# A hybrid mixer and product-key expert block on one Trainium2 core: segments of 1, 2, 2, 3 tiles, eight gather slots, other V rows on TensorE, and a segment's opening among the queries of the one before

## The reference, cut to what matters

```python
h = rmsnorm(x, norm_mix)
gq, gk, gv, gr, ga, sq, sk, sv = split(h @ w_in)
y_gla = gla_branch(gq, gk, gv, gr, ga) @ w_gla_out      # gated linear attention, chunks of 64, state carried
y_swa = swa_branch(sq, sk, sv, sinks) @ w_swa_out       # window of 2 chunks, 16 heads, ALiBi, sinks
gates = sigmoid(h @ w_branch_gate + b)                  # two gates of width 1024
x = x + (g_gla * y_gla + g_swa * y_swa) @ w_out
h = rmsnorm(x, norm_ffn)
q = (h @ w_q)                                           # 8 heads x 2 halves of 128
scores = q . sub_keys                                   # 128 keys in each half
top 16 of each half, top 16 of the 16 x 16 sums -> expert numbers e, gates g = softmax
x = x + sum over 8 heads x 16 experts of g * gelu(h . u_tab[e]) * v_tab[e]
x = x + sigmoid(rmsnorm(x) @ w_ple_gate) * (p @ w_ple_proj)
return rmsnorm(x, norm_final)
```

## Time and profile before

| | us |
|---|---|
| median of 3 runs (3624.73 to 3629.0) | 3628.56 |
| the profiled execution | 3617.58 |
| its span | 3615.5 |
| TensorE, VectorE, ScalarE, GpSimd busy | 2923.2, 2506.4, 1421.8, 1249.0 |
| first gather issued | 233.5 |
| `ysum` of the eight tiles added | 835, 1212, 1630, 2030, 2430, 2830, 3230, 3571 |

### The profile page before, as it was taken

How to read it: one execution, slowest core, us unless ns; L and a number is a source line. 1 busy time by engine, 2 the same in 40 slices (tenths; PEclk the granted TensorE clock), 3 DMA queues, 4 the chain that set the end, 5 groups by cost and what they waited for, 6 DMA issues and landing times.

```text
span 3615.5 us, 35606 instructions
## 1 busy us (share of the span) xinstructions
PE 2923.2 (81%) x11272; PEld 1953.4 (54%) x11272; DVE 2506.4 (69%) x5309; ACT 1421.8 (39%) x3619; POOL 1249.0 (35%) x1028
## 2 busy tenths in 40 slices
PE   8869988869887789587898789787877788686865
PEld 6767766746564456364576456464444455353423
DVE  0155666697778877689777986688666756677773
ACT  2223454233434443344443453344433543334532
POOL 0012222224343444344334443343433433333441
PEclk9989999988999899798899899899998998798988
DMA  6588878979999999999999999999999999999996
GB/s 221 177 334 337 340 315 328 365 305 422 421 421 420 414 390 420 421 393 398 400 421 421 420 403 405 403 414 390 421 421 421 421 421 421 419 398 412 413 421 248
DMA packets 198988, 1388.12 MB, mean 384 GB/s; under 512 B 22657, under 2 KB 24577, under 8 KB 35090
## 3 DMA queue, kind: packets, MB, share of 16 engines
q0 software_dynamic: 147456, 1073.81, 72.3%
q1 hardware_dynamic: 51346, 312.04, 21.8%
HBM read 1368.99 MB, written 16.78 MB: 383 GB/s over the span
## 4 chain that ended last, share of the span: by engine, by line
PE 34%; DMA 32%; DVE 17%; issue 8%; ACT 7%; POOL 2%; SPq 0%; DVEq 0%; POOLq 0%; ACTq 0%
DMA uv<-in_uv,idx 30%; PE bank L540 12%; PE bank L550 9%; PE ysum L728 8%; DVE acc L1241 4%; DVE uv L1218 4%; POOL uv L497 2%; DVE lidx L1077 2%; PE bank L609 2%; DVE vals L1074 1%; ACT bufX L804 1%; DMA slab<-in_slabs 1%; DVE bufE L1071 1%; DMA out<-bufA 1%; PE bank L529 1%
## 5 line engine op out<-in xcount | busy, mean ns | idle before, releaser
L497 POOL DMA_INDIRECT uv<-in_uv,idx x1024 | 1248.8, 1220 | 2299.3 <-PE ysum L728 1061.3
L1218 DVE SCALAR_TENSOR_TENSOR uv<-uv,hbuf 128x1024 f32<-128x1024 f32 x1024 | 1246.2, 1221 | 564.4 <-DMA uv<-in_uv,idx 544.7
L728 PE MATMUL ysum<-uv,diag 128*128 128x512 f32 x2232 | 1169.7, 666 | 402.8 <-ACT diag L974 396.2
L728 PEld LDWEIGHTS ysum<-uv,diag 128*128 128x128 f32 x2232 | 449.1, 211 | 966.5 <-ACT diag L974 533.1
L1241 DVE SCALAR_TENSOR_TENSOR acc<-uv,dots,acc 128x1024 f32<-128x1024 f32 x466 | 595.8, 1279 | 115.2 <-ACT dots L965 109.8
L960 ACT ACTIVATE dots<-dots 128x2 f32<-128x2 f32 x512 | 103.1, 201 | 1150.3 <-DVE uv L1218 1149.0
L540 PE MATMUL bank<-bufA,slab 128*128 128x256 f32 (+1 forms) x2400 | 441.0, 343 | 6.4 <-DMA slab<-in_slabs 3.7
L540 PEld LDWEIGHTS bank<-bufA,slab 128*128 128x128 f32 x2400 | 393.0, 195 | 80.3 <-issue 38.1
L550 PE MATMUL bank<-slab,bufA 128*128 128x256 f32 x1408 | 314.3, 382 | 0.7 <-ACT bufE L761 0.4
L550 PEld LDWEIGHTS bank<-slab,bufA 128*128 128x128 f32 x1408 | 270.0, 192 | 58.6 <-issue 24.1
L965 ACT ACTIVATE dots<-dots,gexp 128x1 f32<-128x1 f32 x1024 | 245.9, 287 | 20.6
(11 more groups left out here) (133 smaller groups left out, 2393.7 us busy)
## 6 DMA issues: line engine op xcount, KB each, us to landing
slab<-in_slabs SPq DMA_DIRECT2D x255, 1024.0 KB, 9.1
uv<-in_uv,idx POOLq DMA_INDIRECT x1024, 15.1
acc<-x_d SPq DMA_DIRECT2D x8, 512.0 KB, 13.3
hbuf<-h_d SPq DMA_DIRECT2D x8, 512.0 KB, 16.1
x_d<-acc SPq DMA_DIRECT2D x8, 512.0 KB, 8.3
bufC<-in_x SPq DMA_DIRECT2D x3, 1024.0 KB, 8.8
bufA<-in_x SPq DMA_DIRECT2D x3, 1024.0 KB, 11.5
x_d<-bufA SPq DMA_DIRECT2D x3, 1024.0 KB, 9.9
```

What stands on the lines that cost most here:

```text
L497: nc.gpsimd.indirect_dma_start(out=uv[:, at % NS, :], out_offset=None, in_=a["uv"], in_offset=bass.IndirectOffsetOnAxis(ap=idx[:, g % 4, k ...
L728: ins = mm(ysum[:, c, :], diag[:, m % DS, :], uv[:, at % NS, D + c * 512:D + c * 512 + 512], start=(m == first), stop=(m == last))
L1218: v.scalar_tensor_tensor(out=row, in0=row, scalar=1.0, in1=hbuf[:, i % HB, :], op0=ALU.mult, op1=ALU.mult, accum_out=dots[:, g % 3, k:k + ...
```

## The change

- `SEGS` becomes (1, 2, 2, 3): four segments, the last with tiles 5, 6 and 7. The five segment buffers grow from two to three tiles. `GROUPS` becomes (0, 1), (2, 3), (4, 5, 6), (7,).
- `NS` goes from 10 slots to 8 and `HB` from 2 to 1, so h of a tile is loaded to `hbuf` only after the last dot of the tile before.
- The rows on TensorE change: none in tile 0 up to row 100 and 12 of 16 behind it, 8 of 16 in tiles 1 and 2, 4 of 16 in tiles 3 and 4, 12 of 16 in tiles 5 to 7, without the last four rows of all. 478 rows instead of 558.
- The first stages of a segment (`OPENING`: `nx`, the new `sc`, which scales x, the turning, and ten pieces) stand among the queries of the segment before, where that segment has no guest; x is then loaded to `bufQ` after `swo3` of the segment before. The decay gate `ga` comes behind these pieces. In a segment with a guest, or at the start, the opening stands ahead of the rest as before.
- At the start SP issues x, two constants and three slabs, and then the other 11 constants; the engines wait for the two, and for the rest only in `ga`.
- The first tile of each segment goes to `acc` by a copy on ScalarE at the end of `hb1`, not through `x1_d`.
- The last tile's x2 is not written and read: the tail works in `acc`. Its `pp` runs 16 steps before the end, its `ysum` is added before the last two V rows, and the product with the gate becomes a stage `mx` of its own.

```diff
-SEGS = (1, 2, 2, 2, 1)
+SEGS = (1, 2, 2, 3)
-NS = 10
-HB = 2
+NS = 8
+HB = 1
-ON_PE = [(1, 4, 7, 10, 13), ODD, ODD, ODD, ODD, MOST, MOST, MOST]
-SPARE = 6
-IS_PE = [at % TOPK in ON_PE[at // (NH * TOPK)] and at % (NH * TOPK) >= SPARE for at in range(ROWS)]
+FEW = tuple(range(3, TOPK, 4))
+ON_PE = [MOST, ODD, ODD, FEW, FEW, MOST, MOST, MOST]
+
+SPARE = [100] + [6] * (NTILE - 1)
+IS_PE = [at % TOPK in ON_PE[at // (NH * TOPK)] and at % (NH * TOPK) >= SPARE[at // (NH * TOPK)] and at < ROWS - 4
+         for at in range(ROWS)]
-GROUPS = ((0, 1), (2, 3), (4, 5), (6,), (7,))
-HOST = {0: 2, 1: 3, 2: 4}
+GROUPS = ((0, 1), (2, 3), (4, 5, 6), (7,))
+HOST = {0: 2, 1: 3}
-TAIL = ["T0", "T1", "pg0", "pg1", "pg2", "pg3", "pp", "T2"]
+TAIL = ["T0", "T1", "pg0", "pg1", "pg2", "pg3", "pp", "mx", "T2"]
+OPENING = ["nx", "sc", "hT0", "hT1", "gk0", "gk1", "gq0", "gq1", "gr0", "gr1", "gr2", "gr3", "sk", "sv"]
+def closing(s):
+
+    wq = [(s, f"wq{j}") for j in range(2, NH + 1)]
     if s in GUEST:
...
+        t = [(GUEST[s], n) for n in TAIL]
+        return [t[0], wq[0], t[1], wq[1], t[2], wq[2], t[3], wq[3], t[4], wq[4], t[5], wq[5], t[6], wq[6], t[7], t[8]]
+    if s + 1 == NSEG:
+        return wq
+    o = [(s + 1, n) for n in OPENING]
+    return [wq[0], o[0], wq[1], o[1], wq[2], *o[2:4], wq[3], *o[4:6], wq[4], *o[6:8], wq[5], *o[8:10], wq[6], *o[10:]]
...
+        if q == LAST_GROUP:
+
+            stand(q, "pp", PER_TILE * NTILE - 16)
+            for i, n in enumerate(n for n in TAIL if n != "pp"):
+                stand(q, n, END + 2 + i)
...
-        xs = by_token_tile(bufC)
+        xs = [by_token_tile(bufC if s - 1 in GUEST else bufQ) for s in range(NSEG)]
...
-                if at == 1 and n == f"wq{NH}" and s + 1 < NSEG:
+                if s + 1 < NSEG and at == 1 and n == (f"wq{NH}" if s in GUEST else "swo3"):
                     sp.wait_ge(bank_full, USES_END[s, n])
-                    sp.dma_start(xs[:, 0:SEGS[s + 1], :], x_rows(s + 1)).then_inc(x_in, 16)
+                    sp.dma_start(xs[s + 1][:, 0:SEGS[s + 1], :], x_rows(s + 1)).then_inc(x_in, 16)
...
+            for dst, src in firsts:
+                sp.dma_start(dst, src).then_inc(first_in, 16)
+            while loaded.n < RS:
+                next_weights()
             for dst, src in consts:
                 sp.dma_start(dst, src).then_inc(const_in, 16)
             for n in range(FIRST, LAST + 3):
                 i, at = divmod(n + 5, PER_TILE)
-                if at == 0 and 0 <= i < NTILE:
+                if at == 0 and i in MOVED:
...
+                    if c == 1:
+
+                        i = AT[s]
+                        if HB > 1:
+                            if i >= HB:
+                                act.wait_ge(dot_done, (i - HB + 1) * NH * TOPK)
+                            fn(hbuf[:, i % HB, :], h2[:, 0, :], ACT.Copy).then_inc(tile_set, 1)
+                        if i >= 2:
+                            act.wait_ge(x2_out[i % 2], 16 * (i // 2))
+                        fn(acc[:, i % 2, :], x1[:, 0, :], ACT.Copy).then_inc(tile_set, 1)
...
+                if n == END:
+                    dve.wait_ge(v_used_dve, DVE_UPTO[ROWS - 2])
+                    add_ysum(NTILE - 1, ysum_added)
```

More of the change, by code:

```diff
@@ L120, in plan, with stand @@
     found = []
+    def stand(of, n, step):
+        at = {name: at for at, o, name in found if o == of}
+        step = max(step, found[-1][0] if found else step, at.get(BEHIND.get(n), step - 1) + 1)
+        found.append((step, of, n))
     for s in range(NSEG):
-        names = [(GUEST[s] if n in TAIL else s, n) for n in front_names(s)]
-        last = [n for _, n in names].index("wq1")
+        names = front_names(s)
+        if not s or s - 1 in GUEST:
+            names = OPENING + names
         due = PER_TILE * AT[s] - AHEAD - 2 if s else AT_ONCE - 2
-        gap = 2 if s in GUEST else 1
+        last = len(names) - 1
         begin = found[-1][0] + 1 if found else due - last
[L127 to L132, removed]
-    for q, tiles in enumerate(GROUPS):
-        if q not in HOST:
+        for i, n in enumerate(names):
+            stand(s, n, begin + i * (due - begin) // last)
+        more, gap = closing(s), 2 if s in GUEST else 1
+        for i, (of, n) in enumerate(more):
+            stand(of, n, due + gap * (i + 1))
+    for q, tiles in enumerate(GROUPS):
+        if q == LAST_GROUP:
+            stand(q, "pp", PER_TILE * NTILE - 16)
+            for i, n in enumerate(n for n in TAIL if n != "pp"):
+                stand(q, n, END + 2 + i)
+        elif q not in HOST:
             begin = max(found[-1][0] + 3, PER_TILE * (tiles[-1] + 1) + 4)
-            found += [(begin + i, q, n) for i, n in enumerate(TAIL)]
+            for i, n in enumerate(TAIL):
+                stand(q, n, begin + 2 * i)
     return found
@@ L201 @@
          for _, s, n in PLAN if n in PIECES]
+MOVED = [i for i in range(NTILE) if i not in AT]
+H_MOVED = MOVED if HB > 1 else list(range(NTILE))
 BATCHES = [sum(2 * t for t in SEGS[:s]) for s in range(NSEG + 1)]
@@ L279, in build @@
         thT = by_feature_tile(bufQ)
-        tp = by_token_tile(bufQ)
+        tp = [by_token_tile(bufC if q == LAST_GROUP else bufQ) for q in range(len(GROUPS))]
         HALF = 512 * TT
@@ L311, in build @@
         acc = sb("acc", [P, 2, D])
+        x2 = [acc[:, (NTILE - 1) % 2:(NTILE - 1) % 2 + 1, :] if q == LAST_GROUP else x1 for q in range(len(GROUPS))]
         diag = sb("diag", [P, DS, P])
@@ L388, in build @@
         ow = uw[0]
+        WRITES = [sum(t > 1 for t in SEGS[:s]) for s in range(NSEG + 1)]
+        H_WRITES = [sum(any(seg_of(i) == r for i in H_MOVED) for r in range(s)) for s in range(NSEG + 1)]
+        SETS = 1 + (HB > 1)
         def vector_done(eng, now, s, n):
@@ L1212, in dot @@
                 if at % (NH * TOPK) == 0:
[L1213 removed]
+                    if i in H_MOVED:
+                        dve.wait_ge(h_in[i % HB], 16 * sum(j % HB == i % HB for j in H_MOVED if j <= i))
+                    else:
+                        dve.wait_ge(tile_set, SETS * AT.index(i) + 1)
                 if g >= 3 and k == 0:
@@ L1238, in add_row @@
                 if m == DVE_UPTO[i * NH * TOPK]:
-                    dve.wait_ge(acc_in[i % 2], 16 * (i // 2 + 1))
+                    if i in MOVED:
+                        dve.wait_ge(acc_in[i % 2], 16 * sum(j % 2 == i % 2 for j in MOVED if j <= i))
+                    else:
+                        dve.wait_ge(tile_set, SETS * (AT.index(i) + 1))
+                if i == NTILE - 1 and m >= DVE_UPTO[ROWS - 2]:
+                    dve.wait_ge(ysum_added, 1)
                 row = acc[:, i % 2, :]
```

169 lines of the change are left out of this document (90 added, 79 removed), and 8 rows, old and new, of the table OPENING.

## The result

The changed kernel takes 3666.1 us (median of 4 runs, 3664.6 to 3676.5) against 3627.0 before: ratio 1.0114, 95% interval 1.0094 to 1.0134. It is 1.1% slower; I had forecast 2.8% less. It moves 1328 MB instead of 1388, as reckoned.

A forecast was written before the change was run, and what follows sets the result against it. TensorE's front part sets the pace through tile 0, DMA bytes from 835 to 3571 us. Stretches 222 + 542 + 805 + 875 + 692 + 347 + 33 = 3516, on the median's scale 3530 us; range 3400 to 3650.

The forecast's parts named there:

- The bytes: Whole kernel: 51 fewer slabs and other saved traffic, together 59.8 MB, worth at most 142 us at 421 GB/s.
- Tiles 5 and 6: No front part left: 46 slabs less, 677 us by bytes plus 15, so 692 us instead of 800.
- Before the first gather: Start of the kernel: 222 us instead of 233, with 5 us from the shorter wait for constants.
- the gate's chain: Before the first gather: moved behind the projections, it fills TensorE idle time and saves 6 us.
- Tile 0: TensorE sets the pace: fewer V rows and two waits (49.0 us) gone, 542 us instead of 602.
- The slots: Tiles 1 and 2: eight slots instead of ten cost 20 us, bounds nothing and plus 200 us.
- hbuf: Single buffer for h: 5 us of lost DMA at each of seven tile ends, bounds 0 and 15.
- my figure of 10 us: Tiles 1 to 4: median landing time of a gather with eight slots, near 10 us instead of 16.2 in tiles 1 and 2.
- rival B: Eight slots starve DMA: landing in tiles 1 to 4 falls only to 13 us, 3695 us in all; chance 0.17.
- Tiles 3 and 4: Three tiles' front beside them, three units needing 739 to 780 us: 875 us instead of 800, bounds 800 and 950.
- Rival C: Tiles 3 and 4 are bound by the front part and take 950 us, 3604 in all; chance 0.12.
- Tile 7 and tail: Tile 7: 333 us for about 140 MB plus 14, so 347; tail: 33 us instead of 44.5.

The follow-up runs named there:

- segs5_8slots: The changed kernel with the old five segments (1, 2, 2, 2, 1) and their groups, still eight slots and one hbuf: 3691.6 us, 1.018 of the kernel before.
- segs5_10slots_odd: The changed kernel with five segments, ten slots, two hbufs and 8 of 16 V rows on TensorE in tiles 3 and 4: 3563.4 us, 0.9827 of the kernel before.
- segs1232: The changed kernel with segments of 1, 2, 3, 2 tiles, V rows and groups moved with them: 3630.9 us, 1.0011 of the kernel before.

## Why the prediction was wrong

**The bytes** came out as worked out: 1328 MB against 1388 less 60. Tiles 5 and 6 lost 46 slabs, 115 us at 2.5 us each, and took 112 us less than before (797 to 685), against 105 forecast with its extras. This agrees with the price of a slab, but it is a net figure and in part luck: against `segs5_8slots`, with the same slots, the stretch lost 144 us. The front that would have needed the slots went with its slabs, and the rate of DMA rose as well (last section); no run parts the three.

**Before the first gather** I had 222 and it took 230. The constants' wait went as said, ScalarE began at 5.8 us instead of 11.4:

```profile
5.77 1.06 ACT L821 ACTIVATE bufX<-bufQ 128x1024 f32<-128x1024 f32 x1
```

but only 3.7 us of that reached the first gather, and the 6 us for the gate's chain did not come.

**Tile 0.** TensorE's work was sized right (500 us against 493 forecast), and both waits of the earlier trace rows are gone. The step that failed is that their 49 us would be saved: of the 89.5 us of idle time before I left 41, and it was 74, so 15 were saved. TensorE now waits in other places, longest for VectorE's results (total, times, longest, 229 to 804 us):

```profile
PE bank L652 <- DVEq L1218: 13.6, 4, 5.1
PE bank L578 <- DVEq L1218: 12.1, 1, 12.1
PE bank L658 <- ACT bufX L814: 11.9, 8, 3.6
PE bank L680 <- ACT aT L814: 10.1, 1, 10.1
```

It is not the slots: `segs5_10slots_odd` takes 580 us here with the same four waits. What a queue stops waiting for at one place it can wait for at the next; a removed wait is an upper bound, not a gain.

**The slots.** I took 20 us in tiles 1 and 2 and had no term for slots in tile 0 and in tiles 3 and 4 but what the 875 holds. I stated 35 us for `hbuf` over seven tile ends, yet the sum does not hold them beside what the stretches lost already: its 14, 15 and 14 us in tiles 1 and 2, 5 and 6, and 7 are hardly more than the 14, 12 and 14 us by which those stretches were longer than their bytes at 421 GB/s. Measured on the kernel before, slots and hbuf cost 96 us by the medians; by stretches of the profiled executions 18, 29, 36, 13 and 11. In tiles 1, 2, 5, 6 and 7 my sizes were about right, and the wait for `hbuf` was 5 us a time as taken, but its price only 9 us. The step that failed here is that tile 0 and tiles 3 and 4 got no term of their own: 18 and 36 us in the kernel before, 32 us in tiles 3 and 4 between the kernels of five segments, and there none in tile 0. A mean time to landing, as I read it from the earlier trace rows, says nothing of the bursts in which slots come free; at 2303 us above, one gather waited 11.7 us, where a cycle of eight slots is some 25 us. That this is the reason is argued, not shown. The time to landing with eight slots cannot be read in these traces, so my figure of 10 us is not tested, and neither is rival B's 13. B's sign was right. Its size was too large (166 us on top of my forecast, where slots and `hbuf` cost 96 to 103 in all), and its place (equal in tiles 1 to 4) was not.

The Trainium skill (Perfetto Trace Analysis, Optimization Strategy) says that the same gap repeating on the engine that should be full can mean too few buffers. The runs agree in part: DMA's share in the kernel before was 1.00 in three stretches with ten slots, and with eight 0.97 in tiles 3 and 4. In tiles 5 and 6 it stayed at 1.00 with eight slots, and the stretch was 13 us longer all the same. None of the runs was searched for a gap that repeats.

**Tiles 3 and 4**, the step that I was least sure of, failed by 96 us and beyond its upper bound of 950. The sum of each unit's work was right within some 5% (TensorE 778 against 739, of which 4 are a slip in the V rows' term; VectorE 750 against 747; DMA 334 MB against 328). The step that failed was to take the largest of three sums (780, DMA) and add a part. Each unit has its own dense times, so the stretch is nearer to the sum over its parts of whichever is the largest there: 915 us in cuts of 40 us, where it took 971. I did this only for TensorE against DMA, for clusters of ten pieces, and left out VectorE's (closing, softmax, the gates' products). The runs show the size of this step without such sums: against `segs5_8slots`, three tiles' front instead of two costs 108 us here, and 90 us beside tiles 1 and 2 in `segs1232`; the slots cost 32 and the V rows moved to VectorE 25 (831 against 806 us in the kernels of five segments and ten slots). Together that is about the 159 us by which the stretch grew (812 to 971), where I had 75. Rival C put the cause in the front part, as the runs do; its price of 950 was too low. This is also why the segment's 127 us shrank to 25: it saved 144 us in tiles 5 and 6 and lost 108 in tiles 3 and 4 and 22 in tile 7.

**Tile 7 and tail.** 373 against 347: I had counted the bytes of the closing group, not its three tiles of TensorE work in one block; the segment's step alone makes it 22 us longer (351 to 373), the slots up to 11. The tail went from 45 to 38 us, 33 forecast.

**How the change adds up**, from the ratios: opening, start, tail and tile 0's V rows minus 1.7% (`segs5_10slots_odd`), V rows of tiles 3 and 4 plus 0.6%, slots and hbuf plus 2.9%, the three-tile segment minus 0.7%: together plus 1.1%. The first part alone, with ten slots and five segments, beats both kernels: 3563 us. The slots were given up for the buffers: in each partition the third tile in five segment buffers is 5 x 4 KB, and two slots and one `hbuf` are 2 x 8 + 4 KB, the same 20 KB. The three-tile segment with more than eight slots was not tried.

**Still open:** how much of the slots' price with eight slots is landing and how much holding; why it grows from one slot to the next; in tiles 3 and 4 the 56 us that the cuts of 40 us do not hold (971 less 915), and how much of them hangs on the order of the queues.

## What to carry to other kernels

When a larger block saves bytes and takes slots for it, price the two apart: here slabs worth 127 us were bought with about 100 us of slots and 100 us of crowding (127 less the 25 that were left). A transfer that is full on average with N slots in flight is not shown to have slots to spare; take one away and measure, it costs one run. Where the sums of three units come near to each other in a stretch (here 739, 747 and 780 us forecast), cut it finely and add up the largest of each cut. The mean of each engine shows room that need not be free at the right time, and even the sum of the largest was here a lower bound (915 of 971 us).

## What the runs showed of the hardware that was not expected

With nothing but gathers the kernel before moved 421 GB/s at most. The changed kernel moved more, here from 2700 to 2800 us:

```profile
2700.00:2800.00 100.00, 71.63 (x125) 27.24 (x124) 73.68 (x144) 33.19 (x102) 49.38 (x42) 0.81 1.01 426
```

This goes with the segment buffers and not with the number of slots. In the 40 slices of their pages all seven kernels with three-tile buffers reach 427 GB/s (`segs1232` too), and the ten with two-tile buffers stop at 421 or 422, with eight, nine and ten slots alike (`segs5_8slots` at 421). With the sizes of the buffers the places of the slots in memory change; which of the two it is no run tells. At a full queue it is 1.4%.

The mean granted clock of TensorE fell from 0.908 to 0.886 with the change. It was 0.85 in tiles 5 to 7, where TensorE idles between V rows, and 0.99 to 1.00 in the cuts in which pieces follow without a gap. In tiles 5 and 6, which lost their front part, it fell from 0.90 to 0.85, and a V row there cost 2.23 us (411.2/184) instead of 2.09 (385.3/184) before: 26 us more of TensorE's time, in a stretch in which it was busy 67%.
